# Dilated mixer: the rests of all ten weight tiles of a step on VectorE

## The reference, cut to what matters

```python
def mixer_a(x, w_in, w_out, cos, sin):
    h = x @ w_in
    for gi, (window, dil) in enumerate(A_GROUPS):        # (128, 1), (512, 4), (2048, 16)
        q, k, v = split_cols_2(h[..., base:base + 3 * A_WIDTH_2], [A_WIDTH_2] * 3)
        q = apply_rope_2(q...)
        k = apply_rope_2(k...)
        o, lse = banded_attention(strided(q), strided(k), strided(v), window // dil)
        ...
    wts = jax.nn.softmax(jnp.stack(lses, axis=0), axis=0)
    o = jnp.einsum('gbsh,gbshd->bshd', wts, jnp.stack(outs, axis=0))
    z = h[..., -A_WIDTH_2:]
    return (o * jax.nn.silu(z)) @ w_out
```

## Time and profile before

| | us |
|---|---|
| median of 3 runs | 1775.49 (1774.39 to 1776.03) |
| the profiled execution | 1770.85 |
| its span, first to last instruction | 1769.6 |
| TensorE busy in the span | 1638.8 |
| VectorE busy | 963.8 |
| ScalarE busy | 647.9 |
| GpSimd busy | 467.9 |

### The profile page before, as it was taken

One profiled execution on the slowest core, in us unless ns is written; L12 is line 12 of the kernel. 1 busy time (PEld: TensorE's weight loads), 2 busy tenths in 40 slices (PEclk: granted clock), 3 DMA queues, 4 the chain that ended last, 5 costly groups with the idle time before them and its releaser, 6 DMA issues.

```text
span 1769.6 us, 24218 instructions
## 1 busy us (share of the span) xinstructions
PE 1638.8 (93%) x9336; PEld 1314.4 (74%) x9336; DVE 963.8 (54%) x1906; ACT 647.9 (37%) x1229; POOL 467.9 (26%) x384
## 2 busy tenths in 40 slices
PE   7999999889999989989899899879999999999888
PEld 5555555358888878846567899878899998878777
DVE  4488888542222277557664788554555444233821
ACT  2442333043333332233333555443444444134511
POOL 1012201015555500022320111015555555013401
PEclk9999999999999999999999999999999999999999
DMA  9334323313222255424432455443444344325131
GB/s 350 113 119 143 103 101 120 131 71 107 96 95 96 95 169 196 159 65 156 148 126 96 155 185 182 155 148 120 132 140 145 134 133 130 125 85 182 60 125 36
DMA packets 63825, 231.16 MB, mean 131 GB/s; under 512 B 7408, under 2 KB 8432, under 8 KB 63456
## 3 DMA queue, kind: packets, MB, share of 16 engines
q1 hardware_dynamic: 60800, 218.65, 36.8%
q0 software_dynamic: 2192, 6.29, 1.1%
q10 hardware_dynamic: 720, 4.68, 0.7%
HBM read 228.55 MB, written 1.05 MB: 130 GB/s over the span
## 4 chain that ended last, share of the span: by engine, by line
PE 84%; DVE 9%; ACT 3%; issue 2%; DMA 1%; POOL 1%; SPq 0%; DVEq 0%; ACTq 0%; POOLq 0%
PE ps L232 17%; PE ps L250 10%; PE ps L251 10%; PE ps L252 10%; PE ps L1193 4%; PE ps L1194 4%; PE ps L1195 4%; PE ps L1623 3%; PE ps L724 3%; PE ps L240 3%; PE ps L714 2%; PE ps L617 2%; PE ps L294 1%; PE ps L1440 1%; PE ps L379 1%
## 5 line engine op out<-in xcount | busy, mean ns | idle before, releaser
L259 ACT ACTIVATE weights_rounded<-ring 128x1024 fp32r<-128x1024 f32 x196 | 205.0, 1053 | 108.2 <-PE ps L1195 108.2
L250 PE MATMUL ps<-h_hi,weights_rounded 128*128 128x512 f32 (+1 forms) x656 | 222.0, 338 | 5.0 <-POOL weights_rest L271 2.9
L251 PE MATMUL ps<-h_lo,weights_rounded 128*128 128x512 f32 (+1 forms) x656 | 221.6, 338 | 0.0
L252 PE MATMUL ps<-h_hi,weights_rest 128*128 128x512 f32 (+1 forms) x656 | 221.5, 338 | 0.0
L265 DVE TENSOR_TENSOR weights_rest<-ring,weights_rounded 128x1024 fp32r<-128x1024 f32 x128 | 175.3, 1371 | 76.2 <-ACT weights_rounded L259 76.1
L271 POOL TENSOR_TENSOR weights_rest<-ring,weights_rounded 128x1024 fp32r<-128x1024 f32 x68 | 163.4, 2405 | 162.7 <-ACT weights_rounded L259 162.7
L232 PE MATMUL ps<-h,ring 128*128 128x512 f32 (+1 forms) x496 | 197.9, 556 | 7.1 <-DVE h L470 7.1
L232 PEld LDWEIGHTS ps<-h,ring 128*128 128x128 f32 x496 | 95.6, 195 | 100.6 <-issue 92.6
L1164 DVE SCALAR_TENSOR_TENSOR scratch<-ps,vectors,scratch 128x510 f32<-128x510 f32 (+1 forms) x88 | 54.1, 615 | 194.6 <-ACT scratch L1124 194.4
L250 PEld LDWEIGHTS ps<-h_hi,weights_rounded 128*128 128x128 f32 x656 | 125.6, 191 | 18.7 <-POOL weights_rest L271 3.3
L1124 ACT ACTIVATE scratch<-ps,vectors 128x512 f32<-128x512 f32 (+1 forms) x88 | 59.1, 672 | 209.6 <-PE ps L252 199.1
(11 more groups left out here) (281 smaller groups left out, 3400.6 us busy)
## 6 DMA issues: line engine op xcount, KB each, us to landing
ring<-in_up SPq DMA_DIRECT2D x88, 512.0 KB, 3.5
ring<-in_ada_rest SPq DMA_DIRECT2D x80, 512.0 KB, 3.5
ring<-in_a_in SPq DMA_DIRECT2D x80, 512.0 KB, 3.5
ring<-in_down SPq DMA_DIRECT2D x44, 512.0 KB, 3.5
ring<-in_even SPq DMA_DIRECT2D x20, 512.0 KB, 3.7
ring<-in_ada_first SPq DMA_DIRECT2D x16, 512.0 KB, 8.7
ring<-in_wout SPq DMA_DIRECT2D x16, 512.0 KB, 3.5
ring<-in_odd SPq DMA_DIRECT2D x16, 512.0 KB, 4.8
```

Source lines behind the costliest of these rows:

```text
L250: te.matmul(bank[:, 0:n], wh[:, k, :], hi(k), start=k == 0, stop=False)
L251: te.matmul(bank[:, 0:n], wh[:, k, :], lo(k), start=False, stop=False)
L252: ins = te.matmul(bank[:, 0:n], wl[:, k, :], hi(k), start=False, stop=k == KD - 1)
L259: sc.activation(pair[0], place(*key), ACT.Copy).then_inc(*mark("rounded", *key))
```

## The change

The rests of tile 9 and of the next step's tiles 0, 1 and 2 go from GpSimd to VectorE. In VectorE's order tile 9's stands ahead of the maxima, the next tile 0's between the maxima and the probabilities, and the next tiles 1 and 2's between the copies of turned probabilities and the gate. GpSimd keeps the three rests ahead of the first step. The semaphores that TensorE and the sync engine wait on follow.

```diff
-    A_POOL = (0, 1, 2, NC - 1)
+
+    def a_on_pool(i, s):
+        return i == 0 and s < 3
+
...
-            tile(("a", i, s), "a_in", NC * i + s, "rest_pool" if s in A_POOL else "rest", "a", i, s)
+            tile(("a", i, s), "a_in", NC * i + s, "rest_pool" if a_on_pool(i, s) else "rest", "a", i, s)
...
-        pe_product3(("a", i, 9), PAIR_A[4], BANK[6], SEQ, xhi, xlo, "rest_pool")
+        pe_product3(("a", i, 9), PAIR_A[4], BANK[6], SEQ, xhi, xlo, "rest")
...
         dve_rope(key, ROPE2, work, TA[0], [at("roped", "a", i, 3)])
+
+        def rest(i, s):
+            if i < KD:
+                dve_rest(("a", i, s), PAIR_A[s % 5], a_free(i, s))
+
+        rest(i, 9)
         dve_maxima(us, HD ** -0.5)
+        rest(i + 1, 0)
         dve_probs(us)
         weigh_copies(ve, 0, A, packs(us), TBA, PTA)
+        rest(i + 1, 1)
+        rest(i + 1, 2)
         dve_gate(A, sga, za)
...
             pool_rope(key, at("copied", *key), QA[x], ROPE2, TA[(x + 1) % 2])
-        rest(i, 9)
-        rest(i + 1, 0)
-        rest(i + 1, 1)
-        rest(i + 1, 2)
```

More of the change, by code:

```diff
@@ L1456, in pe_mixer_a @@
                 te.wait_ge(*at("z_copied", "a", i - 1))
-            pe_product3(("a", i, n), PAIR_A[n % 5], BANK[6 + n % 2], SEQ, xhi, xlo, "rest_pool" if n in A_POOL else "rest")
+            pe_product3(("a", i, n), PAIR_A[n % 5], BANK[6 + n % 2], SEQ, xhi, xlo, "rest_pool" if a_on_pool(i, n) else "rest")
             if n:
```

## The result

The changed kernel takes 1789.26 us (median of 4 runs, 1786.80 to 1791.69) against 1775.67 for the kernel before (4 runs): 1.0076 times as long, 95% interval 1.0061 to 1.0090, 13.6 us slower. The prediction said 1792.6, between 1783 and 1801. The profiled execution took 1789.62.

A forecast was written before the change was run, and what follows sets the result against it. TensorE's in-order queue was taken to bound each mixer step. A stall of 12.3 us plus three clock falls, 4.8, gave 17.1 on the profiled 1770.85, 1788.0; with 4.64 from profile to median, 1792.6 us, range 1783 to 1801.

The forecast's parts named there:

- The bound: Middle mixer step: its length is TensorE's in-order queue, 38.67 us of work in 40, so only TensorE's waits count.
- Tile 9 ahead of the maxima: VectorE at a step's end: the rest waits for its rounding, and the maxima behind it start 1.75 us late.
- Tile 0, and the size of the stall: Between maxima and probabilities: rest from 1309.70 to 1310.93; TensorE's turns delayed 1.55 us in seven steps, 1.45 in the last.
- The extra hundredths for the fourth probability: TensorE's second group of turns needs the fourth probability and was to lose a few hundredths of a microsecond more.
- Tiles 1 and 2: Ahead of the gate, where VectorE idles 4.88 us: these rests cost nothing; without that cover up to 1.23 each.
- the probabilities' lost contention: Without GpSimd's second rest on the shared ports, the four probabilities take 1.79 us in place of 2.29.
- The clock: TensorE's longer idle time at the turns makes its granted clock fall in three steps, 4.8 us in all.
- The neighbours: Similar TensorE waits bounding the falls: lower, second layer's 1.38 and 0.46, none; upper, first layer's 2.01, three of four.
- The sum: Whole kernel: stall of 12.3 us plus clock falls of 4.8 us make 17.1 us slower.
- A: Rival: the stall at the turns without any clock fall, 12.3 us, 1787.8; chance 0.27.
- B: Rival: the stall plus a clock fall in every step, 25.2 us, 1800.7; chance 0.16.
- C: Rival: not slower; half-idle VectorE takes the rests and contention at the turned blocks goes, 2.0 us, 1773.5; chance 0.10.

The follow-up runs named there:

- only9: Changed kernel with the rests of tiles 0, 1 and 2 given back to GpSimd, only tile 9's left on VectorE: 1786.64 us.
- filled: Changed kernel plus eight unread products in every step, between the values product and the turns, filling TensorE's stall: 1787.05 us.
- only12: Changed kernel with the rests of tiles 9 and 0 given back to GpSimd, only those of tiles 1 and 2 left on VectorE: 1777.79 us.
- only0: Changed kernel with the rests of tiles 9, 1 and 2 given back to GpSimd, only tile 0's left on VectorE: 1771.37 us.
- behind: Changed kernel with tile 9's rest moved behind the maxima, still on VectorE ahead of the next tile 0's rest: 1784.27 us.
- nine_back: Changed kernel with tile 9's rest alone given back to GpSimd: 1771.98 us.

## Why the prediction was right, and where its sizes were off

**The bound.** Right: TensorE's work in a step did not change, and each step grew by what TensorE waits at the turns.

**Tile 9 ahead of the maxima.** Right to a hundredth: the rest was worked out to start at 1305.09 and the maxima at 1306.24; on the same clock they start at 1305.10 and 1306.24. Of the 1.75 by which the maxima are late, 0.61 is the wait for the rounding and 1.14 the rest's own time. `only9` has this cost alone: against a step whose probabilities nothing blocks (39.79) it is 1.53 in a middle step.

**Tile 0, and the size of the stall.** Its rest starts at 1309.70, as worked out. The four reciprocals take 0.34 with overlap, not 0.4, so the probabilities start at 1311.10 for 1311.23, and the second turned block goes at 1312.41 for 1312.55. The extra hundredths for the fourth probability were not paid. A middle step grew by 1.37 for 1.55; the last one by 1.52 for 1.45. The stall is 7 x 1.37 + 1.52 = 11.1 where 12.3 was predicted, and `filled`, which has the stall without the falls, has a mixer 11.0 longer than before.

**Tiles 1 and 2.** Right: `only12` has the step of before, and on its clock tile 3's rest ends at 1323.50, as worked out. In the changed kernel's list of TensorE's waits there is no rest and no load.

**What goes the other way.** The prediction counted the probabilities' lost contention (2.29 to 1.79) inside the delay, and the traces agree: of the ten profiles, the 2.29 stand only in the 14 steps (`before`, `only12`) in which GpSimd still makes its second rest when the probabilities start, and there the first of the four alone is longer, 0.91 for 0.40. The Trainium skill (SBUF — State Buffer, "Who interferes with whom") calls the ports that the two engines share an exclusive lock. These rows fit that, though the probability loses 0.50 where GpSimd's rest, whose times are rough, has 0.69 to go. The prediction did not see that the gain, 0.30 a step, was to be had by itself. Taken apart, a middle step is -0.30 for the lifted contention, +1.53 for tile 9, +0.14 for tile 0 behind it, 0 for tiles 1 and 2.

**The clock.** Three falls of 1.6 were taken; the profiles have two and three, and a fallen step is 1.53 to 1.61 longer. The neighbours gave the right bounds, of eight steps neither none nor all, but three was a choice between them, and that it came so near is luck. The lower neighbour was also weaker than it looked. The four waits of the second layer in the trace of before are not alike (two of 1.38 and 0.46, one of 1.38 and 0.89, one of 1.19 and 0.46), and that no clock falls behind them holds in two of the ten profiles only; in the other eight it falls behind the first. The changed kernel's first and second wait show both:

```profile
823.99 0.33 PE L717 MATMUL ps<-consts,big 128*128 128x128 f32 x1 [1.37 <-DVE big L672]
824.78 3.39 PE L717 MATMUL ps<-consts,big 128*128 128x128 f32 x15 [0.46 <-DVE big L672]
...
865.90 1.86 PE L717 MATMUL ps<-consts,big 128*128 128x128 f32 x15 [0.46 <-DVE big L672]
```

Why one step falls and the next, with the same wait, does not stays open.

**The sum.** 17.1 was predicted and 13.6 measured. 1.2 of the excess is the stall. In the profile the sum closes: 11.1 and two falls of 1.6 are 14.3, and the mixer is 14.2 longer. In the median, what remains of the excess cannot be given to a step: two profiles of the changed kernel have mixers 14.2 and 16.6 longer than before, and the medians also hold the other stages, which move by as much.

**The rivals.** A and B differ from the forecast only in the falls, and both are out by the profiles. C is out: the rest would have had to be over when the scores were ready, and it began 0.61 after that.

## What to carry to other kernels

An engine that is half idle still has stretches without slack, and an in-order queue gives a moved instruction's wait and its own time to everything behind it: look up when its input is ready, and what stands behind it at that moment. Here 14 of 29 moves were free, 7 were a gain when alone, and 8 cost 12.2 us, more than the whole stall; giving those eight back made the change faster than the kernel before. When a chain of small steps has no slack, take the waits off it that a bank or a buffer causes: the two left in this step took 7.7 us off the mixer, where the best division of the rests took 2.2.

## What the runs showed of the hardware that was not expected

The granted clock falls behind waits in stages that no edit touched, and not at the same places in each execution. In the ten profiles the stretch behind the mixer, the same instructions each time, takes 248.0 us with 2.8 us given up at half clock (`only0`) to 252.9 with 10.7 (`behind`), the loss being one less the granted clock, added up over the stretch. Two kernels whose mixers differ by 2 us had medians 5 apart (`only0` and before), and falls of this kind can make that difference. Whether a shift of some microseconds ahead of those stages settles how many falls they have, or only chance does, was not tried. Three profiles speak for the shift: `only0`, `nine_back` and `only12` all gave up 41.0 us ahead of the mixer; the first two, whose mixers are equally long, then have two falls each at the same places (78.5 and 245.7 us after the mixer), while `only12`, whose mixer is 2.1 us longer, has five. That is not enough to show it.
